# Modulation vectors in sets of 2048 columns: layer 1's summed on VectorE, layer 2's placed at three norms

## The reference, cut to what matters

```
cond_lat = jax.nn.silu(c)[:, None, :]                   # cond_ctx likewise from c_ctx
sh1, sc1, g1, sh2, sc2, g2 = jnp.split(cond_lat @ w_ada[i] + b_ada[i], 6, axis=-1)
h_lat = modulate(rms_norm(x, norm_gain[i, 0]), sh1, sc1)     # h * (1 + scale) + shift
...
x = x + g1 * o_lat
x = x + g2 * swiglu(modulate(rms_norm(x, norm_gain[i, 1]), sh2, sc2), ffn_w_in[i], ffn_w_out[i])
```

## Time and profile before

| | |
|---|---|
| median of 3 runs | 1762.58 us |
| profiled execution, its own time | 1766.16 us |
| its span | 1764.1 us |
| TensorE matmul busy | 1582.0 us (90%) |
| VectorE busy | 686.9 us (39%) |
| ScalarE busy | 506.7 us (29%) |
| GpSimd busy | 187.3 us (11%) |
| mean granted TensorE clock | 0.954 |
| read from HBM | 386.17 MB, 220 GB/s over the span |

### The profile page before, as it was taken

One profiled execution on the slowest core, in us unless ns is written; L12 is line 12 of the kernel. 1 busy time (PEld: TensorE's weight loads), 2 busy tenths in 40 slices (PEclk: granted clock), 3 DMA queues, 4 the chain that ended last, 5 costly groups with the idle time before them and its releaser, 6 DMA issues.

```text
span 1764.1 us, 21735 instructions
## 1 busy us (share of the span) xinstructions
PE 1582.0 (90%) x8882; PEld 1130.8 (64%) x8882; DVE 686.9 (39%) x1306; ACT 506.7 (29%) x1016; POOL 187.3 (11%) x155
## 2 busy tenths in 40 slices
PE   6799899999999969997899987887699999999896
PEld 2477577777776749986899986786434443434333
DVE  1324522223233368865655555875510101010102
ACT  1322322222233334444444454452200000000001
POOL 0001001101000025400122211130000000000000
PEclk8899999999999979999999998998699999999999
DMA  8741234454455533211255433323299999999993
GB/s 362 286 169 72 98 149 183 167 191 158 176 203 229 222 156 112 105 48 40 84 190 190 156 144 107 120 96 123 93 417 427 426 427 426 427 427 426 426 427 128
DMA packets 53704, 388.69 MB, mean 220 GB/s; under 512 B 5968, under 2 KB 6112, under 8 KB 6880
## 3 DMA queue, kind: packets, MB, share of 16 engines
q1 hardware_dynamic: 53168, 384.57, 55.1%
q10 hardware_dynamic: 432, 2.67, 0.4%
HBM read 386.17 MB, written 1.05 MB: 220 GB/s over the span
## 4 chain that ended last, share of the span: by engine, by line
PE 74%; DVE 11%; DMA 8%; ACT 5%; issue 1%; DVEq 0%; SPq 0%; ACTq 0%; PEldq 0%
PE twin L626 41%; PE twin L1100 15%; DMA ring<-in_wblk 8%; PE twin L595 4%; PE twin L1156 3%; DVE wlo L1695 2%; PE twin L614 2%; PE twin L603 2%; PE twin L683 2%; ACT whi L1252 2%; DVE rst L1724 1%; DVE Hl L1733 1%; PE twin L820 1%; PE twin L1090 1%; PE twin L660 1%
## 5 line engine op out<-in xcount | busy, mean ns | idle before, releaser
L1695 DVE TENSOR_TENSOR wlo<-ring,whi 128x512 fp32r<-128x512 f32 (+1 forms) x306 | 270.9, 910 | 167.3 <-ACT whi L1252 165.5
L626 PE MATMUL twin<-Hh,whi 128*128 128x256 f32 (+1 forms) x864 | 289.4, 335 | 19.7 <-DVE Hl L1733 12.9
L626 PE MATMUL twin<-Hl,whi 128*128 128x256 f32 (+1 forms) x864 | 285.3, 330 | 0.0
L626 PE MATMUL twin<-Hh,wlo 128*128 128x256 f32 (+1 forms) x864 | 285.1, 330 | 0.0
L1100 PE MATMUL twin<-ring,xg 128*64 128x512 f32 x1024 | 227.9, 598 | 16.9 <-ACT xT L1563 8.2
L1252 ACT ACTIVATE whi<-ring 128x512 fp32r<-128x512 f32 (+1 forms) x408 | 224.7, 611 | 59.0 <-PE twin L626 59.0
L1596 POOL TENSOR_TENSOR wlo<-ring,whi 128x512 fp32r<-128x512 f32 x102 | 136.8, 1341 | 968.2 <-ACT whi L1252 968.2
L626 PEld LDWEIGHTS twin<-Hh,whi 128*128 128x128 f32 x864 | 167.2, 194 | 41.0 <-issue 13.7
L626 PE MATMUL twin<-hsp,whi 128*128 128x512 f32 (+1 forms) x704 | 178.0, 344 | 11.3 <-DVE hsp L1803 8.3
L1100 PEld LDWEIGHTS twin<-ring,xg 128*64 128x64 f32 x1024 | 76.2, 137 | 158.5 <-issue 146.3
L626 PEld LDWEIGHTS twin<-Hh,wlo 128*128 128x128 f32 x864 | 167.4, 194 | 14.0
(11 more groups left out here) (313 smaller groups left out, 1899.4 us busy)
## 6 DMA issues: line engine op xcount, KB each, us to landing
ring<-in_wblk SPq DMA_DIRECT2D x362, 1024.0 KB, 9.7
xT<-in_xin ACTq DMA_DIRECT2D x1, 2048.0 KB, 15.5
ring<-in_wblk SPq DMA_DIRECT2D x4, 512.0 KB, 5.0
small<-in_small SPq DMA_DIRECT2D x1, 1122.0 KB, 11.3
out<-hTm SPq DMA_DIRECT2D x1, 1024.0 KB, 3.8
dft<-in_dft SPq DMA_DIRECT2D x1, 640.0 KB, 9.1
cons<-in_cons ACTq DMA_DIRECT2D x1, 421.0 KB, 8.6
cols<-in_cols ACTq DMA_DIRECT2D x1, 134.0 KB, 5.5
```

The source lines that it names most:

```text
L626: t = e.matmul(out, a, b, start=start and n == 0, stop=stop and n == 2)
L1695: e.tensor_tensor(lo, w, hi.bitcast(F32), ALU.subtract).then_inc(*s_lov.up(m, h))
```

## The change

The modulation is cut into 9 sets of 2048 columns instead of 36 pieces of 512, three for each layer. A set is eight blocks of the stream, each with 128 rows of the matrix by 2048 columns. The bytes are the same: 24 blocks for each layer, as before.

- **Layer 0 and layer 2** stay on TensorE: 4 matmuls a block, as before, in the same four column groups, which now hold four different groups of 512 columns. Set 0 is computed around the sums of norm 0; of set 1 two blocks after each quarter of the Fourier transform's first step; of set 2 one after each part of its second. Set 6, 7 and 8 (layer 2) stand at norms 2, 3 and 4: two blocks ahead of the sums, six behind.
- **Layer 1** goes to VectorE: `weigh` multiplies a block of 128 x 2048 by a column of the condition and adds it to a running sum, once for each of the two conditions, in the order of the `fin` blocks of feed-forward 0 (one block of the modulation to each, two more in the first `fout` blocks). After eight blocks TensorE adds up the partitions (`ada_sum`, 8 matmuls).
- Each set has one copy into `arow`, one `ada_cols` (4 matmuls, of 8 columns instead of 2) and one group of bias additions, where four pieces had four.
- The rotation tables and rows that only the attention needs move out of `cons` and `small` into an input of 512 KB, `rope`, which ScalarE's queue loads when feed-forward 0 has ended. GpSimd makes its tables when that has landed.

```diff
-ADA = [(layer, cg) for layer in range(3) for cg in range(12)]
+SETS = [(layer, s) for layer in range(3) for s in range(3)]
...
+STREAM = [("ada", 0, s, k) for s in range(3) for k in range(8)]
+_first = BLK["fin", 0, 0]
+for _m, _t in enumerate(SPLIT):
     STREAM.append(_t)
...
+    if 1 <= _m - _first <= 24:
+        STREAM.append(("ada", 1) + divmod(_m - _first - 1, 8))
+    for _s, _after in enumerate((("din", DIN[0]), ("fin", 1, 0), ("win", WIN[0]))):
+        if _t == _after:
+            STREAM += [("ada", 2, _s, k) for k in range(8)]
...
+            def ada_rows(n, ks):
+                layer, s = SETS[n]
+                for k in ks:
+                    tag = ("ada", layer, s, k)
+                    w = block_of(tag)
                     e.wait_ge(*landed(tag))
+                    if k == 0 and n:
+                        e.wait_ge(*s_arow.at(n - 1))
                     for g in range(4):
...
+                        t = e.matmul(bank[7][32 * g:32 * g + 32, :], cact[:, 1 if layer == 2 else 0, k, :], w[:, g * 512:(g + 1) * 512],
+                                     start=k == 0, stop=k == 7)
+                    t.then_inc(*s_adam.up(n, k))
+
+            def ada_sum(n):
+                e.wait_ge(*s_adv.at(n, 7))
+                e.wait_ge(*s_arow.at(n - 1))
+                for s in range(2):
+                    for g in range(4):
+                        t = e.matmul(bank[7][32 * g:32 * g + 32, :], pick[:, s, :], ada_sums[s][:, g * 512:(g + 1) * 512], start=s == 0, stop=s == 1)
...
             e.wait_ge(*s_cond.at("c2"))
-            rows(0)
-            rows(1)
             e.wait_ge(s_cons, 16)
+            ada_rows(0, range(4))
+            sums(0)
+            ada_rows(0, range(4, 8))
             ada_cols(0)
...
+            ada_rows(6, range(2))
             sums(2)
+            ada_rows(6, range(2, 8))
             for u in range(12):
                 unit(u)
+                if u == 0:
+                    ada_cols(6)
...
+            def weigh(p, s):
+                n, k = 3 + p // 8, p % 8
+                tag = ("ada", 1, p // 8, k)
+                w, c = block_of(tag), cact[:, 0, k, s:s + 1]
...
+                if k == 0:
+                    t = e.tensor_scalar(ada_sums[s], w, c, None, ALU.mult)
+                else:
+                    t = e.scalar_tensor_tensor(ada_sums[s], w, c, ada_sums[s], ALU.mult, ALU.add)
...
+            def ada_fout(j, kk):
+                if j < 2 and kk % 2:
+                    weigh(22 + j, kk // 2)
+                if (j, kk) == (5, 0):
+                    mods(5)
...
+            e.wait_ge(*s_wmm.at(*BEFORE[2]))
+            e.dma_start(rope, rope_d).then_inc(s_rope_in, 16)
             squares(2, lambda c: e.wait_ge(*s_fx.at(0, c, 1)))
             root(2)
             high(2)
+            arow_of(6)
```

More of the change, by code:

```diff
@@ L74, in width @@
     return BW // 2 if tag[0] == "fout" and tag[3] == 5 else BW
-STREAM = [("ada", 0, cg, kh) for cg in range(12) for kh in range(2)]
-_late = [("ada", layer, cg) for layer, cg in ADA[12:]]
-for _t in SPLIT:
+STREAM = [("ada", 0, s, k) for s in range(3) for k in range(8)]
+_first = BLK["fin", 0, 0]
+for _m, _t in enumerate(SPLIT):
     STREAM.append(_t)
-    _k = 0
-    if (_t[0] == "fin" and _t[1] == 0 and _t[2] >= 2 and _t[2] % 2 == 0) or (_t[0] == "fout" and _t[1] == 0):
-        _k = 1
-    if _t == ("din", 0):
-        _k = 2
-    for _ in range(_k):
-        _a = _late.pop(0)
-        STREAM += [_a + (0,), _a + (1,)]
+    if 1 <= _m - _first <= 24:
[3 more added lines that the diff above has]
+            STREAM += [("ada", 2, _s, k) for k in range(8)]
 NPRE = len(STREAM)
@@ L206, in ffn_memory @@
             FSIL.append(own(f"sil{layer}", [P, 2, n]))
+            if layer == 0:
+                stage_sum.append(own("stream_sum", [P, BW]))
             give_back(2)
@@ L703, in pe, with ffn @@
                     t.then_inc(*s_wmm.up("fnet", b, m))
-            def ffn(layer, after_pair, after_block):
+            def ffn(layer, around, after_chunk, after_block):
                 n = FN[layer]
@@ L901, in pe, with around, after_chunk @@
                 attention_out(c, range(KC))
-            ffn(1, lambda bp: None, lambda j: None)
+            def around(x):
+                ada_rows(7, range(2, 8) if x else range(2))
+            def after_chunk(p, m):
+                if (p, m) == (1, 0):
+                    ada_cols(7)
+            ffn(1, around, after_chunk, lambda j: None)
             def project(n):
@@ L1254, in arow_of @@
             def arow_of(i):
[L1255 removed]
+                e.wait_ge(*s_adam.at("rows", i))
                 if i:
@@ L2305, in constants, with rotation @@
     put("nsl", tile(-np.sin(ang) * s))
+    put("ones", np.ones((P, P)))
+    put("causal", np.kron(np.eye(2), np.triu(np.ones((64, 64)))))
+    put("slot", np.tile(np.arange(64), (P, 1)))
+    put("tri", np.triu(np.ones((P, P)), 1))
+    put("iota", np.tile(np.arange(8) - 99.0, (P, 1)))
+    sel = np.zeros((P, 8))
+    for g in range(4):
+        sel[32 * g, 2 * g] = sel[32 * g + 1, 2 * g + 1] = 1.0
+    put("sel", sel)
+    return f, dft
+def rotation():
     inv = (np.float32(10000.0) ** (-np.arange(16, dtype=np.float32) / np.float32(16))).astype(np.float32)
```

256 lines of the change are left out of this document (133 added, 123 removed).

## The result

| | before | changed |
|---|---|---|
| median of the runs | 1762.13 us (1759.62 to 1762.64) | **1691.41 us** (1689.6 to 1695.26) |
| profiled execution, its own time | 1766.16 us | 1692.76 us |
| span, mean granted clock | 1764.1 us, 0.954 | 1690.9 us, 0.96 |

The ratio is 0.9604, with a 95% interval of 0.9584 to 0.9625: 70.7 us less, where 71.4 were forecast (1691 us). A second set of six runs of the changed kernel gave 1692.35 us and 0.9600 [0.9570, 0.9630].

What follows compares the result with a forecast made beforehand. TensorE was taken to bound feed-forward 0, transfers the last 488 us, with TensorE waiting at the norms. 50.6 + 16.5 + 10.1 - 4.2 - 1.6 = 71.4 us saved, from 1762.58 to 1691 us; range 1684 to 1700.

Steps and rivals of the forecast that it cites:

- Feed-forward 0: Modulation pieces leave TensorE and weighings hide on VectorE: 59.7 - 8.55 - 0.5 = 50.6 us saved (43 to 53).
- that rival: VectorE bounds feed-forward 0's input half from a weighing of 3.9 us; at 5.5 all comes to nothing, 1763 us; 2%.
- 0.5 us in `fout`: First two fout blocks: a weighing delays the next chunk's low part at four places, 0.5 us lost in all.
- Start: Sums follow the fourth block at once and the transform stops waiting for pieces 4 and 5: 16.5 us saved (11 to 19).
- Norm 2: Sums end 11.7 us earlier, less the rows, copy and turn behind them: 10.1 us saved (6 to 14).
- It is then paced by VectorE's chunks of 1.6 us and catches up: Norm 2: the first product starts 2 us late behind the rows, but that delay is made up.
- the clock stays up: Rival: TensorE has work where it waited; full speed gives 2.5 us at each norm and the start: 1681 us; 13%.
- Norm 3: Eight blocks, none there before; first product 4.4 us late, some 2.8 caught up: 4.2 us lost (1.6 to 10).
- 1.0 for a slow clock: Norm 3: an allowance of 1.0 us within the 4.2 us lost there.
- Norm 4: TensorE's wait of 9.61 us hides six blocks; copy 0.6 and turn 1.0: 1.6 us lost (-1 to 4).
- Blocks not hidden: Rival: at the norms the ring hands out the later four blocks singly at 4.7 us each: 1707 us; 18%.
- Contention: Rival: VectorE and GpSimd delay each other; 5.6 us in fout gives 1697, with fin blocks losing too 1710; 7%.

Runs made afterwards that it cites:

- e1: Changed kernel with layer 1's three sets back on TensorE as rows behind feed-forward 0's first 24 blocks, VectorE weighing nothing: 1713.73 us, ratio 0.9737.
- e2: Changed kernel with each layer 1 block weighed three times instead of twice on VectorE, the extra pass adding zero: 1698.33 us, ratio 0.9637.
- e3: Changed kernel with each layer 1 block weighed four times on VectorE, two extra passes adding zero: 1736.78 us, ratio 0.9857.
- e5: Changed kernel with set 2's copy, turn and bias moved into the middle of the first projection: 1691.63 us, ratio 0.9592.
- e9: The changed kernel unaltered, run again beside e10 and e11 as reference: six runs from 1687.44 to 1696.89 us.
- e11: Changed kernel with the edits of e5, e6 and e10 together: 1680.78 us, ratio 0.9539.
- e6: Changed kernel with the 22nd block's second weighing moved behind the low parts of the first two hidden chunks: 1687.59 us, ratio 0.9568.
- e7: Changed kernel with no rows at norm 3: set 7 at norm 4, set 8 behind the mixer's projections 1 to 4: 1691.37 us, ratio 0.9579.
- e8: Changed kernel with set 6's eight blocks behind feed-forward 0's last eight fout blocks, none at norm 2: 1698.55 us, ratio 0.9635.
- e10: Changed kernel with six blocks instead of eight at norm 2, four at norm 3, the others in feed-forward waits: 1688.92 us, ratio 0.9581.

## Why the prediction was right

**Feed-forward 0, 50.6 forecast, 52.4 found.** A pair at 21.81 for 21.9, the weighing 2.34 for 2.40, the wait behind the last `fin` block 3.85 for 3.9, the wait between the halves 1.97 for 3.2 (the two-deep low parts are made ahead, 1.2 us better). e1 shows the mechanism from the other side, e2 that the cover in the `fin` half is real, and e3 where it ends. The prediction had put that point at a weighing of 3.9 us. In e3 a weighing with its double is 4.7, and 4 x (4.7 - 3.9) x 11 pairs = 35 us is what the input half lost (34.6, its end included): that rival's mechanism was right, its condition not met. What the prediction had at 0.5 us in `fout` cost nothing: behind the last `fin` block TensorE has no wait but the one between the halves. But that room is all used, since e2's extra pass arrives in full.

**Start, 16.5 forecast, 15.6 found.** The transform began at 40.12 (before 43 forecast) and its first quarter ended at 46.31 instead of 48 to 48.5: the lead was 18.1 us at the transform's end. Then set 2's copy, turn and bias, which stand ahead of the first split, took 2.5 back. I had written that both versions have 54.5 us to the end of the second step, and had stopped looking there; e5 shows what stands behind it.

**Norm 2, 10.1 forecast, 11.7 found.** The sums came 12.3 us earlier (11.7 forecast), ending 9.1 behind the last product. Then TensorE was free 10.2 us behind the sums, not 8.5 to 9, since the last blocks come 2.48 us apart. "It is then paced by VectorE's chunks of 1.6 us and catches up" did happen: of the 11.7 us, 8.8 are the shorter wait, 2.5 are caught up by the 24th product, and 0.4 lie in the rest of the attention. The step at norm 2 was right, and a little more came of it than forecast.

**The rival "the clock stays up"** had 2.5 us at each norm and 2.5 at the start. Behind norm 2 the clock was indeed higher than before (0.80 and 0.89 for 0.63), but behind the 24th product that gave 0.4 us in the changed kernel's first profile and 2.4 in its second (e9), and e11 had as much with fewer blocks (1.5). As far as these executions show, that was a matter of the execution and not of the blocks at norm 2. At one place the changed kernel lost clock instead: behind the last `fin` block, where the prediction put the wait of 3.85 us at its length alone (e6).

**Norm 3, 4.2 lost forecast, 6.3 found, with a term mis-sized.** e7 prices the eight blocks there at 6.0 (3.7 by the executions at full clock). The wait for the ring was foreseen, but the first product came 10.3 us behind the sums where the blocks were to end at 8.5. It started 7.0 us later than before, against the last product, and the 24th 5.4 later: 1.6 came back and not 2.8. In e5, with the clock at 1.00 there, it started 6.0 later and the 24th 3.2: there 2.8 came back, as forecast, and the stretch to the first product of hidden chunks was 4.1 us longer than before, against 6.4 in the changed kernel's profile. So the number 4.2 fits the executions at full clock, in part by luck, since the blocks ended 0.8 us later than forecast and the 1.0 for a slow clock was not needed; for the others that 1.0 was too small.

**Norm 4, 1.6 forecast, 0.9 found**, and 1.5 in e9.

**What was luck.** That 70.7 us were measured and 71.4 forecast is closer than the terms are. Start and norm 1 were 1.4 short, feed-forward 0 1.8 over, norm 2 with the attention 1.6 over, norm 3 2.1 short, norm 4 0.7 over, and two stretches whose products the change leaves alone, the mixer and the end, gave 2.1 and took 1.0. The profiled executions differ by 73.4 us and the medians by 70.7.

**The rivals.** "Blocks not hidden" was half right in mechanism and far off in price: norm 3 lost 6.3 where that rival had 10, since blocks land 2.48 apart and not 4.7. "Contention" exists and costs nothing in `fin`. The groups by shape for 186 to 420 us (busy us, mean ns of one, idle before) are, in the changed kernel and in e1, which weighs nothing:

```profile
L1739 DVE TENSOR_TENSOR wlo<-ring,whi 128x512 fp32r<-128x512 f32 x63 | 59.2, 978 | 30.4 <-ACT whi L1291 30.4
L1642 POOL TENSOR_TENSOR wlo<-ring,whi 128x512 fp32r<-128x512 f32 x21 | 42.3, 2016 | 189.2 <-ACT whi L1291 189.2
```

```profile
L1739 DVE TENSOR_TENSOR wlo<-ring,whi 128x512 fp32r<-128x512 f32 x57 | 50.6, 913 | 92.3 <-ACT whi L1291 91.9
L1642 POOL TENSOR_TENSOR wlo<-ring,whi 128x512 fp32r<-128x512 f32 x19 | 24.6, 1297 | 205.7 <-ACT whi L1291 205.7
```

GpSimd's quarter takes 2.02 us on average instead of 1.30 when VectorE weighs beside it: of the 21 there, 11 took 1.29 and 10 took 2.81. A weighing is 2.34, but 3.40 in two cases, both in `fout`, and both started 0.05 us behind a GpSimd quarter of 1.29. The Trainium skill (SBUF — State Buffer, Who interferes with whom) has the two exclude each other for the length of an instruction, and these rows agree with such waiting on both sides. GpSimd has one quarter in 11 us, so it has the time. In `fout` TensorE does not wait for it either.

## What to carry to other kernels

Before moving work onto an engine "with room", look at the room by stretch: the same pass of 2.35 us was free 22 times in `fin` blocks and cost its whole length in each `fout` block, where buffers are two deep. A block of filler work at a norm adds to the wait for the first product, but where the products behind it are paced by another engine's chunks, most of that is caught up; read its price at the point where TensorE no longer waits for chunks, and not at the first product (4.3 us there, 1.8 at the 24th). A wait that is added ahead of a dense stage can cost more than its length: 3.85 us instead of 1.58 brought up to 2.4 us of lower clock behind it. And before a difference of a stage is put down to an edit or to the clock, split the stage, and look at other executions whose code is the same there. And price interleaved work by a row where it stands alone between products (1.20 us), not by one from a run of the same kind (0.93).

## What the runs showed of the hardware that was not expected

- The granted clock behind norm 2 goes with what TensorE did ahead of it. With all eight blocks of rows there, the first 20 us behind the first product had 0.72 to 0.97 in ten executions, with fewer or none 0.63 to 0.68 in four (before, e8, e10, e11). The time does not follow: behind the 24th product the attention took 199.5 to 202.5 us in the ten and 200.4 to 202.2 in the four.
- A short wait can lower the clock behind it: with TensorE idle 3.85 us ahead of the output half of feed-forward 0 the granted clock fell there in nine of nine executions (0.73 in the 10 us behind the wait in the changed kernel), with 0.59 to 2.19 us in none of five.
- The same code differs from one execution to the next with the clock: 209.9 and 206.0 us for the attention of the changed kernel; from the attention's end to feed-forward 1's last product 220.2 to 220.5 us in five executions, 217.0 in one and 215.5 to 215.6 in three. A profile's stage is good to some 5 us there, though to 0.1 us in places that run at the same clock (255.07 and 255.09 for the input half of feed-forward 0 in the changed kernel and e9).
- A block of 1 MB takes 4.7 us from issue to landing, but with several under way they arrive every 2.48 us, some 420 GB/s, while each of them then takes longer (9.7 us for the one issued at 797.08 in the changed kernel).
